# Sliding sums of the pool group: from GpSimd to VectorE, between two recurrence levels, in a hybrid decoder block

## The reference, cut to what matters

```python
POOL_WINDOWS = (2, 4, 8, 16)      # 4 groups of 64 channels
def pool_mixer(v, w_grp, scale):
    ...
    for gi, w in enumerate(POOL_WINDOWS):
        lo = jnp.pad(cs[:, :S - w + 1, gi], ((0, 0), (w - 1, 0), (0, 0)))
        cnt = jnp.minimum(t + 1, w).astype(f32)[None, :, None]
        pooled.append((cs[:, 1:, gi] - lo) / cnt)
    pooled = jnp.stack(pooled, axis=2) - vf
    y = jnp.einsum('bsgc,gcd->bsgd', pooled, w_grp.astype(f32)).reshape(B, S, POOL_WIDTH)
    return (y * scale.astype(f32)).astype(v.dtype)
```

## Time and profile before

| | |
|---|---|
| median of 3 runs | 2506.2 us (2505.4 to 2508.0) |
| the profiled execution: its time | 2504.1 us |
| its span (first to last instruction) | 2502.3 us |
| mean granted TensorE clock | 0.972 of full |
| TensorE matmuls busy | 2340.2 us (94%) |
| VectorE busy | 1295.1 us (52%) |
| ScalarE busy | 752.0 us (30%) |
| GpSimd busy | 330.1 us (13%) |

### The profile page before, as it was taken

The page is one execution under the profiler, slowest core; times in us unless marked ns, Lnnn a source line. Parts: engine busy times, 40 slices in busy tenths (PEclk is TensorE's granted clock), DMA queues, the critical chain, the costliest instruction groups (busy, mean ns, idle before and its releaser), DMA issues.

```text
span 2502.3 us, 33301 instructions
## 1 busy us (share of the span) xinstructions
PE 2340.2 (94%) x11307; PEld 1906.5 (76%) x11307; DVE 1295.1 (52%) x2143; ACT 752.0 (30%) x1472; POOL 330.1 (13%) x234
## 2 busy tenths in 40 slices
PE   5798989999999889999999998999999988999997
PEld 5777668788778678888878767888878857888885
DVE  6746568384855735243445645425255573515345
ACT  1143543233333532122124343212123253211112
POOL 3334134444313000000000200000000300000000
PEclk9898999999999999999999999999999989999998
DMA  8765168878754234655545323655546413555554
GB/s 305 270 220 218 55 217 303 298 276 296 268 212 159 85 135 171 229 189 190 196 160 211 135 86 147 228 195 186 191 153 230 151 50 135 221 209 191 188 190 176
DMA packets 115205, 483.11 MB, mean 193 GB/s; under 512 B 7808, under 2 KB 38794, under 8 KB 69514
## 3 DMA queue, kind: packets, MB, share of 16 engines
q1 hardware_dynamic: 115081, 481.53, 53.1%
HBM read 378.74 MB, written 102.76 MB: 192 GB/s over the span
## 4 chain that ended last, share of the span: by engine, by line
PE 84%; DVE 8%; ACT 4%; issue 3%; DMA 1%; SPq 0%; DVEq 0%; ACTq 0%
PE ps L586 17%; PE ps L588 17%; PE ps L587 17%; PE ps L603 8%; PE ps L602 8%; PE ps L604 8%; PE ps L654 2%; PE ps L620 1%; DVE AA L1290 1%; DMA AW<-in_w_ada_dram 1%; ACT SM L1079 1%; DVE SM L1432 1%; PE ps L741 1%; PE ps L707 1%; DVE st L1420 1%
## 5 line engine op out<-in xcount | busy, mean ns | idle before, releaser
L586 PE MATMUL ps<-hTh,wt 128*128 128x512 f32 x1920 | 752.6, 392 | 7.8 <-DVE hTl L1354 5.6
L588 PE MATMUL ps<-hTh,wt 128*128 128x512 f32 x1920 | 748.4, 390 | 0.0
L587 PE MATMUL ps<-hTl,wt 128*128 128x512 f32 x1920 | 748.4, 390 | 0.0
L586 PEld LDWEIGHTS ps<-hTh,wt 128*128 128x128 f32 x1920 | 361.2, 188 | 85.6 <-issue 9.6
L588 PEld LDWEIGHTS ps<-hTh,wt 128*128 128x128 f32 x1920 | 361.1, 188 | 76.0
L587 PEld LDWEIGHTS ps<-hTl,wt 128*128 128x128 f32 x1920 | 361.2, 188 | 74.1 <-issue 0.5
L1561 DVE TENSOR_SCALAR cv<-ub,CW 128x512 f32<-128x512 f32 x176 | 106.4, 605 | 475.4 <-ACT ub L1192 460.6
L1192 ACT ACTIVATE ub<-ps 128x512 f32<-128x512 f32 x176 | 105.1, 597 | 701.9 <-PE ps L588 701.9
L603 PE MATMUL ps<-wt,pTl 128*128 128x512 f32 x704 | 280.7, 399 | 0.0
L602 PE MATMUL ps<-wt,pTh 128*128 128x512 f32 x704 | 278.9, 396 | 0.0
L604 PE MATMUL ps<-wt,pTh 128*128 128x512 f32 x704 | 277.0, 393 | 0.0
(11 more groups left out here) (213 smaller groups left out, 2568.7 us busy)
## 6 DMA issues: line engine op xcount, KB each, us to landing
wt<-split_w SPq DMA_DIRECT2D x268, 1024.0 KB, 4.8
split_w<-wt SPq DMA_DIRECT2D x88, 1024.0 KB, 7.0
AW<-in_w_ada_dram SPq DMA_DIRECT2D x12, 2048.0 KB, 9.1
raw<-in_w_up_dram SPq DMA_DIRECT2D x22, 1024.0 KB, 9.6
XN<-in_x_dram SPq DMA_DIRECT2D x5, 2048.0 KB, 9.2
raw<-in_w_in_dram SPq DMA_DIRECT2D x8, 1024.0 KB, 11.7
XT<-in_x_dram SPq DMA_DIRECT2D x4, 2048.0 KB, 9.4
raw<-in_w_down_dram SPq DMA_DIRECT2D x8, 1024.0 KB, 9.3
```

Source lines behind the costliest of these rows:

```text
L586: mm(ps[:, slot, :], w, hTh[:, k, :], start=(k == 0), stop=False)
L587: mm(ps[:, slot, :], w, hTl[:, k, :], start=False, stop=False)
L588: ins = mm(ps[:, slot, :], wl[:, slot, k, :], hTh[:, k, :], start=False, stop=(k == KD - 1))
```

## The change

The sums go to VectorE, in two calls of a new function `window_sums(a)`: the groups with windows 2 and 4 (a = 0) behind `level_mul(2)`, those with windows 8 and 16 (a = 1) behind `level_mul(3)`, each ahead of the `level_take` that follows. The division goes into the weights (`PW`, once, ahead of the blocks), so that scaling and subtraction are one instruction, `y - w * PV`, by a new column `nwcol` of the negative windows (four more memsets on GpSimd at the start). GpSimd's list in blocks 1 to 3 is empty; in block 0 it only makes low parts of weights. Nothing changes on TensorE, ScalarE and the load queue.

```diff
@@ GpSimd, start
                 step(pool.memset(wcol[sl, i // 2:i // 2 + 1], float(w)))
+                step(pool.memset(nwcol[sl, i // 2:i // 2 + 1], float(-w)))
@@ GpSimd, each block
-                step(pool.tensor_tensor(PV[:, :, 0:16], PVc[:], one, ALU.mult))
-                pool.wait_ge(s["qe_ready"], b + 1)
-                pool.wait_ge(s["level_taken"], b * 13 + 1)
...
-                    step(pool.tensor_tensor(cur[:, 1:], x_[:, 1:], x_[:, 0:E_ - 1], ALU.add))
...
-                step(pool.tensor_tensor(R[:], R[:], PV[:, :, 16:], ALU.subtract))
...
-            with pool.Fori(1, NB) as b:
-                one_block(b, False)
@@ VectorE, start
-                pre_(V.tensor_copy(PW[r, :, r], PW32[r]))
+                pre_(tt(PW[r, :, r], PW32[r], invw[r].unsqueeze(2).to_broadcast([64, 2, 64]), ALU.mult))
@@ VectorE, each block
+                def window_sums(a):
+
+                    if a == 0:
+                        dve.wait_ge(s["acc_taken"], eb_ + 10)
+                        step(ts(PV[:, :, 0:16], PVc[:], 1.0, None, ALU.mult))
+                    cur, nxt = (y[:].rearrange("p a n -> p (a n)")[:, 0:E_] for y in (O, T1))
+                    x_ = PV[:, a, :]
+                    step(tt(cur[:, 1:], x_[:, 1:], x_[:, 0:E_ - 1], ALU.add))
+                    for n, w in enumerate((2, 4, 8)[:3 if a else 1]):
+                        r = slice(64, 128) if n == 2 * a else slice(0, 128)
+                        step(tt(nxt[r, 2 * w - 1:], cur[r, 2 * w - 1:], cur[r, w - 1:E_ - w], ALU.add))
+                        cur, nxt = nxt, cur
+                    for r, y in ((slice(0, 64), nxt), (slice(64, 128), cur)):
+                        step(tt(y[r, 16:32], y[r, 16:32], corr[r, a, :], ALU.mult))
+                        ins = stt(R[r, a, :], PV[r, a, 16:], nwcol[r, a:a + 1], y[r, 16:], ALU.mult, ALU.add)
+                        if a and r.start:
+                            ins.then_inc(s["pool_ready"], 1)
+                        else:
+                            step(ins)
+                    if a:
+                        step(ts(corr[:].rearrange("p a n -> p (a n)"), ones[:, 0:32], 1.0, None, ALU.mult))
+                        step(ts(PVc[:], PV[:, :, BT:BT + 16], 1.0, None, ALU.mult))
@@ VectorE, the loop over the levels
                     if o + 1 < len(LEVELS):
                         level_sub(o + 1)
                         level_mul(o + 1)
+                    if o in (1, 2):
+                        window_sums(o - 1)
```

More of the change, by code:

```diff
@@ L61 @@
 ADA_DVE = 6
-ACT_STEPS, DVE_STEPS, UP_STEPS, POOL_STEPS = 28, 92, 16, 17
+ACT_STEPS, DVE_STEPS, UP_STEPS = 28, 108, 16
 def place(u):
@@ L149, in hymba_block @@
         wcol = sb("wcol", [P, 2])
+        nwcol = sb("nwcol", [P, 2])
         corr = sb("corr", [P, 2, 16])
@@ L459, in _ @@
                     .then_inc(s["t32_split"], 1)
-            n_pre = step.n
             def one_block(b, first):
-                ub_, eb_ = b * UNITS, b * EVACS
+                ub_ = b * UNITS
                 def refill(base, u):
@@ L471, in one_block @@
                     refill(ub_, u)
-                step = Steps(pool, s["pool_steps"], b * POOL_STEPS + n_pre)
-                pool.wait_ge(s["acc_taken"], eb_ + 10)
-                one = ones[:, 0:32].rearrange("p (a n) -> p a n", a=2)
-                step(pool.tensor_tensor(PV[:, :, 0:16], PVc[:], one, ALU.mult))
-                pool.wait_ge(s["qe_ready"], b + 1)
-                pool.wait_ge(s["level_taken"], b * 13 + 1)
-                WA, WB = (y[:].rearrange("p a n -> p (a n)")[:, 0:E_] for y in (O, T1))
-                for a in range(2):
-                    x_, cur, nxt = PV[:, a, :], WA, WB
-                    step(pool.tensor_tensor(cur[:, 1:], x_[:, 1:], x_[:, 0:E_ - 1], ALU.add))
[L483 to L490, removed]
-                step(pool.tensor_tensor(R[:], R[:], PV[:, :, 16:], ALU.subtract))
-                step(pool.tensor_tensor(corr[:], one, one, ALU.mult))
-                pool.tensor_tensor(PVc[:], PV[:, :, BT:BT + 16], one, ALU.mult).then_inc(s["pool_ready"], 1)
-                assert step.n == POOL_STEPS, step.n
                 if first:
```

## The result

The changed kernel takes 2512.1 us (median of 18 runs, 2510.6 to 2531.5); the kernel before, run beside it on the same chips, 2506.2 us. The ratio is 1.004, with a 95% interval of 1.0024 to 1.0056: slower by 0.4%, or 10 us (the ratio compares runs of the same round on the same chip; the two medians over all rounds differ by 5.9). The forecast was 0.8% slower, 2526.8 us. The sign and the new waits were forecast rightly. So the question of this study is where the other 10 us went.

What follows compares the result with a forecast made beforehand. TensorE, busy 94% of the span, was taken to bound the kernel. Waits 9.7, clock 3.0, block 0 7.9 + 1.7 - 1.7 make +20.6 us: 2506.2 to 2526.8, range 2515 to 2538 (2511 to 2538 for 8 in 10).

Steps and rivals of the forecast that it cites:

- What bounds the kernel: Whole kernel: TensorE's matmuls are busy 94% of the span; in the level stretch TensorE waits for nobody.
- the room at `level_take(3)`: Blocks 1 to 3: 2.02 us before TensorE's KG transposes, against 5.2 us of window_sums(1); new wait 3.2 us each, 9.7 together.
- `window_sums(0)` hidden: Behind level_mul(2), blocks 1 to 3: 3.6 us of sums end as level_take(2) starts, with nothing left over; costs TensorE nothing.
- Block 0: Sums meet GpSimd's weight work at level_take(3): wait 7.9 us, clock 1.7; a 1.7 us wait in the attention goes.
- The clock at the wait: Behind new waits in blocks 1 to 3, TensorE's clock may halve, losing 1.7 us each: 3.0 us in all, bounds 0 and 5.1.
- The sum: Whole kernel: 9.7 (waits) + 3.0 (clock) + 7.9 + 1.7 - 1.7 (block 0) = +20.6 us.
- The heads: Attention, first reduction to O: 23.5 us in block 1, 29.2 in block 3 with the same instructions; called sensitive to the clock.
- cards dealt anew: Attention's head: a shift of 3 to 8 us may change its length; allowed 4 us less, 6 more in the range.
- rival 1: At the KG transposes, blocks 1 to 3: the wait stays under half of 3.2 us; 2511 to 2515 us, chance 0.08.
- Rival 2: No difference: sums lie in VectorE's idle time, GpSimd's sums were off the path; 2506 us, chance 0.04.
- Rival 3: Faster: VectorE operations stretched by GpSimd's sums were on the path, 13 us in three blocks, 1.7 in block 0; 2491, chance 0.03.
- Rival 4: Much slower: waits bring the clock down each time, in block 0 twice, attention's heads fall badly; 2538 to 2548 us, chance 0.10.

Runs made afterwards that it cites:

- e5: The changed kernel with window_sums(1) alone moved between level_sub(5) and level_mul(5); window_sums(0) stays. 2504.5 us, ratio 0.9985.
- e4: The kernel before without the sums, correction and subtraction; GpSimd only gives its signal. 2501.8 us, ratio 0.9984.
- a2: The changed kernel unaltered, profiled a second time. 2520.6 us, one run.
- e2: The changed kernel without the tensor nwcol (wcol negated in place), so all tensors lie where they lay before. 2526.7 us, ratio 1.0083.
- f1: The changed kernel with 14 unused matmuls of constants filling TensorE's wait ahead of the KG transposes. 2521.8 us, ratio 1.0065.
- e1: The kernel before plus one unused tensor of 8 bytes where the change puts nwcol; no instruction differs. 2500.2 us, ratio 0.9967.
- e6: The kernel before plus an unused tensor of 96 bytes, so pTh and pTl lie at multiples of 128 bytes. 2497.7 us, ratio 0.9963.
- e7: The kernel before with 13 unused matmuls of constants in TensorE's wait ahead of the attention's scores(2), every block. 2509.0 us, ratio 1.0006.

## Why the prediction was right, and by half wrong

**What bounds the kernel, and the room at `level_take(3)`: right.** The forecast read 2.02 us of room where 5.2 us of sums were put, and a wait of 3.2. One reading was too broad: the earlier trace rows begin at 1385, and ahead of that, from 1326 on, TensorE waits twice in block 2's level stretch, 0.7 and 1.2 us for ScalarE. These waits are older than the sums and are the same after, so nothing hangs on them. The trace has sums of 5.3 and a wait of 3.45 in each of blocks 1 to 3. The 0.23 that is missing is the pause between the last sum and the copies, which the sum of durations left out. The 0.05 us for the signal stood on no row; from the copies' end to the transposes it is 0.13 in block 1.

**`window_sums(0)` hidden: right.** e5 leaves it in place, and the level stretch is that of before. The cover was just as thin as read: `level_take(2)` now starts behind the sums and not behind TensorE.

**Block 0: right.** Wait 7.91 us (forecast 7.9), level stretch +9.8 (forecast 7.9 + 1.7 = 9.6). The collision came earlier than forecast and hit an operation of 16 columns, but it cost the same. The head gained 1.5 us in e4 (forecast 1.7). The 9.0 us that the high bound takes for this wait stand on no row; they did not come. The page "SBUF — State Buffer" of the Trainium skill (Who interferes with whom) says that a VectorE instruction with two SBUF inputs contends with a GpSimd instruction that reads SBUF, and that the shared ports are an exclusive lock. The trace agrees: the correction takes 2.35 us instead of 0.17, beside a GpSimd instruction of 2.34.

**The clock at the wait: right in kind, too small.** The forecast took 3.0 us, as if somewhat over half of three waits brought the clock down. All three did, in after, a2 and e2 alike. By f1 it is 1.6 us for each wait, and by subtraction in after 98.5 - 93.2 - 3.45 = 1.85: 5 to 5.6 us for the three. So the move costs the level stretch 25.8 us, where the terms of the sum for it are 22.3.

**"The sum" had a term missing: this is the step that failed.** The prediction listed waits, clock, block 0 and the memsets, and took everything the change does not touch as unchanged. The new tensor was read as an operand of an instruction and not as 32 bytes of memory, by which `pTh` and `pTl` move. e1 measures that term alone at -0.33% (-8 us; -4 to -13 by the interval), and the matmul starts give up to -9.4. The counterpart, e2, has the change without the term: +20.7 us, where the forecast for exactly that was +20.6. From e2 to after it is 0.43%, near all of what the forecast was off. That e2 meets the forecast to 0.1 us is luck: its level stretch is 26.2 us longer than before, 3.9 more than forecast, and the other stretches gave as much more back. No row of the trace of before shows this term. What could have been seen is that matmuls of one shape start every 0.232 to 0.2365 us with `pTh` and `pTl` and every 0.227 elsewhere, a difference that asks for a cause.

**The heads: a second term, too small.** The prediction gave 4 us less and 6 more for the "cards dealt anew" and put only the 1.7 us of block 0 into the sum. The profiled execution gave -9.5. In the medians it must be less, since e2's heads stand only 1.3 us under those of before and a2 has one long head. As a ledger: +25.8 of level stretch and -8 of placement make some +17.5, and +10 was measured. The other 7 or so lie in the rest of the kernel, by the profiles in the heads, where 1.7 was forecast. With intervals of 4 us on both the +10 and the -8, the medians can't tell how the part that is missing divides between heads and placement.

**The rivals.** The measured 2512 us lies among the times of rival 1 (2511 to 2515), but rival 1's mechanism is refuted, as the wait is 3.45 us and not under half of 3.2. A time that fits a theory does not bear it out. Rival 2 fell at the room of 2.02 us, as it said it would. Rival 3: the stretched subtractions went back to 1.23 us and brought nothing, and by e4 all that could be had is some 4 us. Rival 4 had one half right, the clock fell at every wait; but it needed long heads too, and in the first profile they were short.

**Open.** Why the stationary operand's address sets the distance of the matmuls. What decides between a short and a long head, and whether the wait in the level stretch really favours the short one: 9 of 12 against 5 of 28 is a strong count, but the heads of one execution may hang together, no experiment set it at will, and f1, with the wait and without the fall of the clock, has two of four. Whether the runs of the changed kernel at the upper end (2527.7 to 2531.5) are those with four long heads: 4 x 4.7 = 19 us would fit, but none of them was profiled. Where the rest of the 4 us that e4 gained lies.

## What to carry to other kernels

Work moved to an engine that is half idle is free only inside its gaps. Find the instruction behind it that a busy engine waits for, and compare the room there (2.02 us) with the work (5.3 us). Where a change adds or removes a tensor, however small, look at where the tensors behind it come to lie, and compare against a version with the same placement. And measure the upper bound of a gain by leaving the work out (e4: 4 us) ahead of asking where to put it.

## What the runs showed of the hardware that was not expected

- The distance of the starts of 128x512 float32 matmuls differs with the address of the stationary operand in its partition: 0.232 and 0.2365 us at 32 past a multiple of 64 bytes, 0.228 and 0.231 at a multiple of 64, 0.227 at a multiple of 128. With 2112 such matmuls the kernel before gains 0.33% (e1) and 0.37% (e6) by its median.
- One stretch of the attention has two lengths, 8.6 or 13.5 us, with the same instructions, at a granted clock of 1.00 or 0.57. Four of them in a kernel could make a spread of up to 19 us (an estimate, 4 x 4.7).
- A wait of 3.45 us with dense matmuls on both sides brought the clock to half each time (9 of 9 in after, a2 and e2), at 1.6 to 1.85 us beyond the wait.
- With 13 or 14 more matmuls in the loop's body, TensorE pauses in the first unit of blocks 2 and 3, for 2.5 us each time in f1 and 1.5 and 2.0 in e7, and the pause shows nothing that it waits for. The turns are 7.2 us longer in f1, which outweighs the 5 us that the filled gap gained. The cause is open.
- The stretch ahead of the blocks takes 130.3 to 134.8 us in kernels in which it is the same but for a few small instructions, and 131.2 and 133.7 in two executions of the changed kernel, so a start that is 3.5 us shorter is no gain of a change.
